# Splitting a stage's first weights during the end of the stage before it, and taking gate and up in turn in the first gated unit

## The reference, cut to what matters

```python
def rms_norm(x, g):
    y = xf * lax.rsqrt(jnp.mean(xf * xf, axis=-1, keepdims=True) + NORM_EPS)
...
def hier_moe(xn, ...):      # 32 experts, all computed, weighted by cw
    hid = silu(xn @ w_gate[e]) * (xn @ w_up[e]);  y += (hid * cw[:, e]) @ w_down[e]
def swiglu(h, w_in, w_out): # 22 units of 128 columns
    a, b = jnp.split(h @ w_in, 2, axis=-1);  return (jax.nn.silu(a) * b) @ w_out
```

## Time and profile before

| what | value |
|---|---|
| median of three runs (lowest, highest) | 4406.94 us (4406.71, 4414.47) |
| profiled execution: its own time, its span | 4407.91 us, 4406.1 us |
| busy PE, DVE, ACT, POOL | 3966.8, 2775.8, 1760.8, 1453.6 us |
| mean granted TensorE clock | 0.895 of full speed |
| bytes moved | 664.40 MB, mean 151 GB/s |

### The profile page before, as it was taken

How to read it: one execution, slowest core, us unless ns; L and a number is a source line. 1 busy time by engine, 2 the same in 40 slices (tenths; PEclk the granted TensorE clock), 3 DMA queues, 4 the chain that set the end, 5 groups by cost and what they waited for, 6 DMA issues and landing times.

```text
span 4406.1 us, 69783 instructions
## 1 busy us (share of the span) xinstructions
PE 3966.8 (90%) x29036; PEld 3589.8 (81%) x29036; DVE 2775.8 (63%) x5143; ACT 1760.8 (40%) x3006; POOL 1453.6 (33%) x804
## 2 busy tenths in 40 slices
PE   7998997979979899979898998989898989799889
PEld 6657996679979886769898967989868989767689
DVE  4446776567767666557776946777647643765542
ACT  3233443434435443224444633444344443432243
POOL 2003443034425432025443421535304444420144
PEclk9658998689989998979999978999869999879899
DMA  5103662146636520016575413757415744310143
GB/s 200 50 37 136 247 248 99 53 158 234 250 138 258 210 102 25 1 58 262 211 275 200 151 56 110 278 208 273 179 64 218 268 155 161 106 39 1 43 157 112
DMA packets 63690, 664.40 MB, mean 151 GB/s; under 512 B 7056, under 2 KB 7568, under 8 KB 7952
## 3 DMA queue, kind: packets, MB, share of 16 engines
q1 hardware_dynamic: 63376, 659.94, 39.8%
HBM read 658.86 MB, written 1.05 MB: 150 GB/s over the span
## 4 chain that ended last, share of the span: by engine, by line
PE 78%; DVE 16%; ACT 3%; issue 2%; POOL 0%; DMA 0%; SPq 0%; DVEq 0%; ACTq 0%
PE pb L269 75%; PE pb L276 3%; DVE wp L226 2%; DVE wk L238 2%; ACT wp L264 2%; DVE wk L226 2%; DVE sq L226 2%; DVE sq L238 1%; DVE hT L238 1%; DVE ada_acc L238 1%; ACT wk L264 1%; DVE xT L238 1%; DVE nt L226 1%; DVE hx L238 0%; DVE hT L232 0%
## 5 line engine op out<-in xcount | busy, mean ns | idle before, releaser
L269 PE MATMUL pb<-hx,wp 128*128 128x256 f32 x15744 | 2014.7, 289 | 91.8 <-DVE hx L226 54.3
L269 PEld LDWEIGHTS pb<-hx,wp 128*128 128x128 f32 x15744 | 1968.4, 196 | 118.4 <-issue 78.5
L226 POOL TENSOR_TENSOR wp<-ring,wp 128x1024 fp32r<-128x1024 f32 (+1 forms) x606 | 1286.9, 2141 | 2252.2 <-ACT wp L264 2252.2
L264 ACT ACTIVATE wp<-ring 128x1024 fp32r<-128x1024 f32 x936 | 940.5, 1046 | 328.2 <-PE pb L269 246.2
L226 DVE TENSOR_TENSOR wp<-ring,wp 128x1024 fp32r<-128x1024 f32 (+1 forms) x650 | 770.5, 1201 | 372.1 <-ACT wp L264 371.2
L269 PE MATMUL pb<-ex,wp 128*128 128x256 f32 x5856 | 754.9, 286 | 2.1 <-DVE ex L226 2.1
L269 PEld LDWEIGHTS pb<-ex,wp 128*128 128x128 f32 x5856 | 721.0, 193 | 23.1 <-issue 20.6
L238 DVE SCALAR_TENSOR_TENSOR ada_acc<-ring,cact,ada_acc 128x384 f32<-128x384 f32 x576 | 530.2, 984 | 58.1 <-ACT ada_acc L264 58.1
L269 PE MATMUL pb<-wk 128*128 128x128 f32 (+8 forms) x3136 | 497.2, 330 | 15.6 <-ACT wk L264 6.2
L269 PEld LDWEIGHTS pb<-wk 128*128 128x128 f32 (+4 forms) x3136 | 346.3, 193 | 162.2 <-issue 98.1
L226 DVE TENSOR_TENSOR sq<-sq,pb 128x256 f32<-128x256 f32 (+1 forms) x360 | 161.6, 449 | 351.7 <-ACT sq L264 304.4
(11 more groups left out here) (175 smaller groups left out, 3010.5 us busy)
## 6 DMA issues: line engine op xcount, KB each, us to landing
ring<-weights SPq DMA_DIRECT2D x385, 1536.0 KB, 6.6
ring<-weights SPq DMA_DIRECT2D x41, 1024.0 KB, 4.9
ring<-weights SPq DMA_DIRECT2D x4, 512.0 KB, 10.2
cst<-consts SPq DMA_DIRECT2D x1, 2032.0 KB, 11.8
ring<-weights SPq DMA_DIRECT2D x1, 1280.0 KB, 5.5
prm<-params SPq DMA_DIRECT2D x1, 1258.0 KB, 7.3
ring<-weights SPq DMA_DIRECT2D x1, 1152.0 KB, 4.9
xT<-xT_in SPq DMA_DIRECT2D x1, 1024.0 KB, 4.8
```

Source lines behind the costliest of these rows:

```text
L226: return self.real.tensor_tensor(out, a, b, op) if self.real else Uncounted()
L264: return self.real.activation(out, a, func, bias=bias, scale=scale, accum_out=accum)
L269: return self.real.matmul(out, l, r, start=start, stop=stop, skip_group_check=skip)
```

## The change

The first pieces of the next stage (`stages[st + 1].first`, by `early`) are split by ACT, DVE and POOL at the end of the current stage: in an FFN or MoE stage in the last unit, ahead of its hidden values; in the others at the last output group. The splits at the start of every stage but stage 0 are gone, with their wait for `x_new`. The wp slots of each gated stage start at a number given by hand (`slot0`), and the three pieces of unit 0 are now split by "v", "vg", "g" instead of "g", "g", "g". After stages whose scratch data overlaps wp, `after` names an earlier event. In unit 0 PE takes gate and up for one tile of x before it goes to the next tile. In MoE stages ACT's hx waits for the end of the stage before as a whole.

```diff
     def gated_dve(e, lin, l):
         for g in lin.groups:
-            split_lo_v(e, g.due)
+            split_lo_v(e, g.due if g is not lin.groups[-1] else early(lin.st + 1))
...
+    def early(st):
+        return stages[st].first if st < len(stages) else []
...
-        fetch(("g", "g", "g"))
+        fetch(("v", "vg", "g"))
...
         def products(u):
             key = (st, "glu", u)
             ps = bk.take(e, key, (v_out, key))
+            if u == 0:
+                pair = g.pieces[u][0:2]
+                for p in pair:
+                    split_ready(e, p)
+                for k in range(KD):
+                    for sig, event in ready(k):
+                        e.wait_ge(*sig[event])
+                    for b, p in enumerate(pair):
+                        ins = mm3(e, ps[:, b * T:(b + 1) * T], part((p.hi, p.lo), k * 128), in_hx(k), k == 0 == b,
+                                  k == KD - 1)
+                ins.then_inc(*product.up(("used", pair[0].at), ("used", pair[1].at), key))
+                return
...  glu_act; the same in glu_dve with split_lo_v
             elif u + 1 < g.units and u != g.first or g.first == 0 == u:
                 split_hi(e, g.pieces[u + 1])
+            elif u + 1 == g.units:
+                split_hi(e, early(st + 1))
...  glu_pool
+        split_lo_g(e, early(g.st + 1))
...  the other stages
-            due_hi(e, l_out)
+            last_hi(e, l_out)
-            due_lo_g(e, l_out)
+            last_lo_g(e, l_out)
...
         def act(e):
-            split_hi(e, A.w.first)
             norm_act(e, st)
...  moe, act
-            split_hi(e, G_.pieces[0][0:2])
             for k in range(KD):
-                e.wait_ge(*x_new[st - 1, k])
+                e.wait_ge(*x_new[st - 1, 7])
                 e.act(Hh[:, k, :], X3[:, k, :], ACT.Copy, scale=gain(k)).then_inc(*x_hi.up((st, "h", k)))
-            split_hi(e, G_.pieces[0][2:3])
...
-    moe(1, 0)
+    moe(1, 0, 0, (x_lo, (0, "o", 7)))
...
-    ffn(11, 1, 2, 1)
-    ffn(12, 2, 0, 0)
+    ffn(11, 1, 2, 1, 3, (summed, (10, "squares")))
+    ffn(12, 2, 0, 0, 1)
```

More of the change, by code:

```diff
@@ L631, in only_split, with last_hi, last_lo_g @@
         return run
+    def last_hi(e, lin):
+        due_hi(e, lin)
+        split_hi(e, early(lin.st + 1))
+    def last_lo_g(e, lin):
+        due_lo_g(e, lin)
+        split_lo_g(e, early(lin.st + 1))
     due_hi, due_lo_v, due_lo_g = only_split(split_hi), only_split(split_lo_v), only_split(split_lo_g)
@@ L801, in ada_mods_dve, with stage, plan_glu @@
              ALU.add).then_inc(*v_ada.up(("mods", i)))
-    units_seen = [0]
-    def plan_glu(st, units, first, unit):
+    stages = []
+    def early(st):
+        return stages[st].first if st < len(stages) else []
+    def stage(st):
+        s = Stage()
+        s.st = st
+        assert st == len(stages)
+        stages.append(s)
+        return s
+    def plan_glu(st, units, first, unit, slot0, after):
         g = Stage()
         g.st, g.units, g.first, g.pieces, g.ada, g.summed = st, units, first, [], {}, {}
+        slot = itertools.count(slot0)
         def fetch(bys):
@@ L815, in fetch @@
             for j, by in enumerate(bys):
[L816 to L819, removed]
-        fetch(("g", "g", "g"))
+                g.pieces[u].append(piece(c.dst[:, j * PIECE:(j + 1) * PIECE], c, next(slot) % NPIECE, by, after))
+        fetch(("v", "vg", "g"))
         pend = None
@@ L953, in glu_dve @@
                 split_lo_v(e, g.pieces[u + 1])
+            elif u + 1 == g.units:
+                split_lo_v(e, early(st + 1))
             if g.ada.get(u) is not None:
@@ L1446, in pool @@
             split_lo_g(e, w_out.first)
-            due_lo_g(e, l_out)
+            last_lo_g(e, l_out)
+        stages[st].first = w.first
         A.w, A.l_out, A.pe, A.dve, A.act, A.pool = w, l_out, pe, dve, act, pool
@@ L1513, in pool, with moe @@
         def pool(e):
-            split_lo_g(e, A.w.first)
             A.pool(e)
         S.pe, S.dve, S.act, S.pool = pe, dve, act, pool
-    def moe(st, l):
+    def moe(st, l, slot0, after):
         S = stage(st)
@@ L1527, in unit @@
             return np.concatenate([a, b, np.asarray(I["moe_w_down"])[l, u]], 1)
-        G_ = plan_glu(st, 32, 2, unit)
+        G_ = plan_glu(st, 32, 2, unit, slot0, after)
+        S.first = G_.pieces[0]
         o = 0
@@ L1687, in pool, with ffn @@
                 e.tt(Q3[:, k, :], X3[:, k, :], X3[:, k, :], ALU.mult).then_inc(*g_step.up((st, "square", k)))
-            split_lo_g(e, G_.pieces[0][2:3])
             glu_pool(e, G_)
         S.pe, S.dve, S.act, S.pool = pe, dve, act, pool
-    def ffn(st, l, s, w):
+    def ffn(st, l, s, w, slot0, after=None):
         S = stage(st)
@@ L1699, in unit @@
                                    ktiles(wi[:, 2816 + u * 128:2816 + (u + 1) * 128]), wo[u * 128:(u + 1) * 128]], 1)
-        G_ = plan_glu(st, 22, 0, unit)
+        G_ = plan_glu(st, 22, 0, unit, slot0, after)
+        S.first = G_.pieces[0]
         def pe(e):
@@ L1736, in ple @@
         ph, pl = ex[:, 0:512], ex[:, 512:1024]
-        w = Weights(st, range(8), (x_new, (st - 1, 7)), (D, D, lambda I, n0, n1: np.asarray(I["ple_w_gate"])[l][:, n0:n1]),
+        w = Weights(st, range(8), None, (D, D, lambda I, n0, n1: np.asarray(I["ple_w_gate"])[l][:, n0:n1]),
                     (D, 256, lambda I, n0, n1: np.asarray(I["ple_w_proj"])[l][:, n0:n1]), ahead=4)
+        S.first = w.first
         l_gate, l_proj = w.lin("gate"), w.lin("proj")
@@ L1753, in dve @@
             for g in l_proj.groups:
-                split_lo_v(e, g.due)
+                split_lo_v(e, g.due if g is not l_proj.groups[-1] else early(st + 1))
                 for m in g.ms:
@@ L2053, in act @@
                 e.act(yh(m), xsT[:, m, :], ACT.Copy).then_inc(*x_hi.up((st, "o", m)))
-            due_hi(e, l_out)
+            last_hi(e, l_out)
         def pool(e):
-            split_lo_g(e, w.first)
             due_lo_g(e, l_conv)
```

54 lines of the change are left out of this document (18 added, 36 removed).

## The result

| | kernel before | changed kernel |
|---|---|---|
| median of four runs each (lowest, highest) | 4409.41 us (4406.71, 4414.47) | **4300.78 us** (4292.01, 4305.83) |
| ratio, 95% interval | | 0.9752 [0.9734, 0.9769] |
| profiled execution: its own time, its span | 4407.91, 4406.1 us | 4305.83, 4304.0 us |
| mean granted TensorE clock | 0.895 | 0.909 |
| busy PE, DVE, ACT, POOL | 3966.8, 2775.8, 1760.8, 1453.6 us | 3936.6, 2751.3, 1763.6, 1423.1 us |

The kernel is 108.6 us faster by the medians; 82 us had been forecast. The profiled execution of the changed kernel is the longest of its four, so the two profiles differ by 102.1 us. All lines of the changed kernel's profile are two higher: L226 is L228, L269 is L271.

A forecast was written before the change was run, and what follows sets the result against it. TensorE's work and waits bound the kernel, the largest wait being 165.4 us for DVE's sq at stage starts. Terms summed to 81.9 us off 4407.9, so 4326 and a median of 4325; range 4302 to 4356.

The forecast's parts named there:

- MoE starts: Stages 1 and 4: with POOL squaring first, then splitting, all tiles come at 352.5 instead of 359.7; gain 11 us each.
- MoE to PLE: Boundaries into stages 2 and 5: gain 7.8 us less 2.4 for later hidden values of unit 31, net 5.4 each.
- PLE to MoBA; PLE to FFN 6: Ends of PLE, short of room for splits: gain 1.3 us into MoBA, -0.1 into FFN 6, where x is 4.4 later.
- RWKV starts; Mamba start: Starts without splits, squares following each tile of x: gain 7.2 us at each of two RWKV starts, 6.3 at Mamba's.
- FFN 8, 9, 11, 14, 15, 17: Starts of these six FFN stages, with the splits gone: gain 4.3 us each, 25.8 in all.
- order of products in FFN: Gate and up in turn in unit 0: nothing in stages 6 to 14, 0.6 us each in 15 and 17.
- stage 12: Start gain of 4.3 us less 7.1 of idle PE and 2.9 of half clock at stage 11's end: -5.7.
- SWA: Stage 13's start: gain 10.0 us less 4.1 lost at the end of stage 12, net 5.9.
- both bad ends: Ends of stages 11 and 12, where early pieces wait for wp slots: cost 7.1 plus 2.9 us, and 4.1 us.
- rival A: All five free gated ends pay like 12 to 13, 4.1 us each, 20 in all, so 4345; chance 0.15.
- The sum: Step adding the terms of all stages to 81.9 us saved, giving 4326 for the profiled execution and 4325 for the median.
- What the splits cost: Stage starts: without POOL's splits, adds end at 2180.4, norm sums take 1.84 us; 4.3 us gained per FFN start.

The follow-up runs named there:

- e4_pool_later: Kernel before, with POOL's three splits at an FFN start held until the sums over features are through PE: 4399.25 us.
- e3_slots: Changed kernel with stage 12 starting at slot 5 and passing over one slot at its pieces 12, 24, 36 and 48: 4289.03 us.
- e5_fifth: Changed kernel with stage 12's slots renumbered, plus SWA's fifth first piece split after the last hidden values of stage 12 instead of before: 4286.72 us.

## Why the prediction was off

The terms of the sum, beside what the two profiles show at their place:

| term | forecast | measured | from |
|---|---|---|---|
| MoE starts | 22 | 26.6 | boundaries 14.9 + 11.7 |
| MoE to PLE | 10.8 | 10.2 | boundaries 17.4, bodies -4.3 and -2.9 |
| PLE to MoBA; PLE to FFN 6 | 1.3; -0.1 | 2.2; 0.1 | boundaries 4.7, 4.3; bodies -2.6, -4.2 |
| RWKV starts; Mamba start | 14.4; 6.3 | 15.3; 6.4 | boundaries |
| FFN 8, 9, 11, 14, 15, 17 | 25.8 | 28.2 | boundaries 4.3 to 5.1 |
| order of products in FFN | 1.2 | 2.6 | body 15: 1.3; stage 17: 1.3 |
| stage 12 | -5.7 | -4.2 | boundary 4.3, body 11 -8.5 |
| SWA | 5.9 | 4.5 | boundary 10.0, body 12 -5.5 |
| sum of the terms | 81.9 | 91.8 | unrounded values added |
| bodies of 0, 3, 7, 10, 13, 16 | 0 | 10.4 | -3.0, -1.1, 4.5, 8.4, 1.6, 0.1 |

**Right.** That the time sits in the starts of stages, that POOL's splits make the adds slow (e4_pool_later), every term within 1.5 us but two, both bad ends with their cause (e3_slots, e5_fifth), that down(0) holds the order of products in FFN, and that no other gated end pays: rival A would have needed five more waits of 4.1 us, and the bodies of stages 6, 8, 9 and 14 stand still. That x comes 4.2 us later behind PLE 5, 4.4 forecast.

**Wrong: the step "The sum".** It takes every stage body as fixed: what a body does by itself stands in the sum at nothing, without a reason, and for Mamba and RWKV the bound is "-1 each". That is what failed. Mamba's body measured 8.4 us less and RWKV 7's 4.5 less. Without Mamba's 8.4 us the median would be about 4309 by this estimate, inside the range. The experiments show that the first is no work of the change. In the kernel before and the four kernels built on it, in which no line of Mamba's body differs, it took 314.1, 313.8, 300.6, 307.1 and 299.3 us, where nothing had been done but to reorder unit 0 or hold POOL in FFN stages, or to put subtractions in front; and it is 299.2 or 299.3 us with and without the change when the granted clock is 0.92. RWKV 7's body scatters likewise, 422.2 us in e4_pool_later and 426.5 in the kernel before, 422.0 and 425.6 in the changed kernel and its repeat, 428.2 in e3_slots. NSA's body, 3.0 us longer in the changed kernel, is scatter of the same kind (302.4 to 311.3 us). MoBA's is not: it took 146.05 to 146.23 us in the five profiles without the early splits and 147.0 to 147.3 in the eight with them, a cost of 1.1 us that the prediction had put at nothing ("no cost"). The profile of the kernel before has the longest Mamba of all thirteen, so that any shift of stage 10 could hardly but gain; that is a reading of the list, not a rule that a run tested.

**Mis-sized.** "MoE start (twice)": 11 forecast, 14.9 and 11.7 measured; unit 0 ended 10.8 and 13.8 us after x, where 14 was forecast. The tiles came at 352.55, where 352.5 was forecast from an x at 340.08; but x was 3.2 us later in that execution, so they took 9.3 us, not 12.4. I had let POOL make all eight squares after x; seven were made while x still came, so that POOL was in DVE's way for the last tile alone. "What the splits cost": the norm sums were taken at the half clock's 1.84 us, and in part of the starts they ran in 1.02; six FFN starts gave 28.2 us, not 25.8.

The median's difference is 6.5 us above that of the two profiles: the profiled execution of the changed kernel, 4305.8 us, lies inside the predicted range, and the median does not. The changed kernel's own four runs go with the clock: 4292.0 us at 0.913, 4300.2 and 4301.4 at 0.910, 4305.8 at 0.909.

**Open.** In Mamba the granted clock is back at 1.00 about 176 us after the first mark in e3_slots and about 219 us after it in the kernel before. That its course there repeats with the same program and changes with edits elsewhere is shown, by one or two profiles of each kernel; by what rule it does is not. That MoE's ACT could take hx tile by tile instead of behind the whole x was not tried: attention's last product reads hx until then.

## What to carry to other kernels

Work that prepares a stage belongs into the slack at the end of the one before, if its buffers are free by then: count the slots at every boundary, since one boundary in seventeen with the wrong start number cost 8.5 us in the body before it, and other numbers gave 7.0 of it back. After such a move, ask again whom the moved work meets: GpSimd's splits beside VectorE's last tiles still cost 3.7 and 4.8 us at the two MoE starts, and one semaphore wait took them back. Where a long stretch runs at a changing TensorE clock, compare the same stretch in several kernels before crediting a change with it, and give the forecast a term of that size: here 22 us in one stage.

## What was unexpected of the hardware

- The same 1872 matmuls of Mamba's body took 292.4 to 314.1 us, with a mean granted clock of 0.95 to 0.87. In the kernel before, the light matmuls of its heads ran at 0.50 for 20 us at a PE that was busy 20.00 of 20.00 us; in e3_slots the same stretch ran at 1.00. In the kernel with 3.4 us of work put ahead of the stage it was 14.8 us shorter, in the one with 1.7 us it was 7.0 us shorter.
- It is not only VectorE's operations with two tensor inputs in SBUF that POOL's splits hold up. A TENSOR_SCALAR, hT<-xT,prm, with one tensor input, took 1.44 us beside them and 0.35 without them, and the Newton step nt<-nv took 2.02 us for 0.17. The Trainium skill, "SBUF — State Buffer", section "Who interferes with whom", names `tensor_scalar` among the operations that can enter a two-port mode and then contend; the trace agrees.
